# Weight panels cast in two halves, with a signal each, in a float32 kernel of three transformer blocks

## The reference

```python
x = first_block(x, p, rel_bias, ...)    # chunked mLSTM and differential attention, gated merge, conv FFN, PLE gate
x = second_block(x, l0_norm_2, ...)     # stick-breaking attention, MLA
return third_block(x, c_3, ...)         # adaLN: SwiGLU, gMLP unit and forgetting attention, SwiGLU
```

## Time and profile before

| | |
|---|---|
| median of 3 runs | 2626.04 us (2624.31 to 2631.66) |
| the profiled execution's own time | 2632.99 us |
| its span, first to last instruction | 2631.0 us |
| PE / ACT / POOL / DVE busy, share of the span | 94% / 39% / 38% / 50% |
| mean granted TensorE clock | 0.973 of 2.4 GHz |
| casts: 128 x 2048 | 188, and one of 128 x 1024 |
| POOL pieces | 754, mean 1367 ns |

### The profile page before, as it was taken

One profiled execution on the slowest core, in us unless ns is written; L12 is line 12 of the kernel. 1 busy time (PEld: TensorE's weight loads), 2 busy tenths in 40 slices (PEclk: granted clock), 3 DMA queues, 4 the chain that ended last, 5 costly groups with the idle time before them and its releaser, 6 DMA issues.

```text
span 2631.0 us, 31263 instructions
## 1 busy us (share of the span) xinstructions
PE 2477.1 (94%) x11720; PEld 1987.5 (76%) x11720; DVE 1324.2 (50%) x1870; ACT 1023.2 (39%) x1327; POOL 1007.3 (38%) x758
## 2 busy tenths in 40 slices
PE   7999899899999899998988899999989989999999
PEld 5887677688887678776766678888869657688886
DVE  6456667866667661444446662222373544522224
ACT  5445576422222543665446542222253433322222
POOL 3332244445554443222443244444424104344442
PEclk9999899999999999999989999999989998999999
DMA  3221496222222122101221122222212102122221
GB/s 137 81 75 54 167 365 261 103 96 96 96 96 96 66 84 75 49 33 50 95 96 64 35 84 96 99 99 98 96 57 93 49 17 80 48 97 96 98 99 57
DMA packets 35957, 245.52 MB, mean 93 GB/s; under 512 B 3951, under 2 KB 4079, under 8 KB 7188
## 3 DMA queue, kind: packets, MB, share of 16 engines
q1 hardware_dynamic: 30096, 207.12, 21.9%
q10 hardware_dynamic: 5764, 37.06, 3.7%
HBM read 242.06 MB, written 2.11 MB: 93 GB/s over the span
## 4 chain that ended last, share of the span: by engine, by line
issue 55%; POOL 28%; PE 15%; DVE 1%; DVEq 0%; POOLq 0%; ACT 0%; ACTq 0%
POOL WL L286 28%; PE PS L316 5%; PE PS L318 5%; PE PS L317 5%; PE PS L1030 0%; PE PS L377 0%; DVE X L2429 0%; DVE ARENA L2424 0%; POOLq L290 0%; DVEq L2095 0%; DVE ARENA L1771 0%; DVEq L2428 0%; PE PS L382 0%; DVE ARENA L1746 0%; POOLq L283 0%
## 5 line engine op out<-in xcount | busy, mean ns | idle before, releaser
L286 POOL TENSOR_TENSOR WL<-WT,WH 128x512 fp32r<-128x512 f32 x754 | 1007.1, 1367 | 1587.9 <-ACT WH L1054 1069.4
L316 PE MATMUL PS<-HH,WH 128*128 128x512 f32 x1568 | 623.2, 397 | 33.8 <-POOL WL L286 10.3
L317 PE MATMUL PS<-HL,WH 128*128 128x512 f32 x1568 | 615.7, 393 | 0.0
L318 PE MATMUL PS<-HH,WL 128*128 128x512 f32 x1568 | 615.6, 393 | 0.0
L1386 ACT CAST WH<-WT 128x2048 fp32r<-128x2048 f32 x90 | 171.9, 1910 | 603.8 <-PE PS L316 603.8
L316 PEld LDWEIGHTS PS<-HH,WH 128*128 128x128 f32 x1568 | 297.7, 190 | 110.4 <-DVE HL L1780 14.6
L316 PE MATMUL PS<-YH,WH 128*128 128x512 f32 x840 | 334.1, 398 | 24.6 <-DVE YL L2559 6.6
L318 PEld LDWEIGHTS PS<-HH,WL 128*128 128x128 f32 x1568 | 297.5, 190 | 63.6
L317 PEld LDWEIGHTS PS<-HL,WH 128*128 128x128 f32 x1568 | 297.9, 190 | 59.6 <-issue 0.2
L318 PE MATMUL PS<-YH,WL 128*128 128x512 f32 x840 | 329.9, 393 | 0.0
L317 PE MATMUL PS<-YL,WH 128*128 128x512 f32 x840 | 329.8, 393 | 0.0
(11 more groups left out here) (305 smaller groups left out, 3350.8 us busy)
## 6 DMA issues: line engine op xcount, KB each, us to landing
WT<-weights SPq DMA_DIRECT2D x188, 1024.0 KB, 4.8
ARENA<-w_ada ACTq DMA_DIRECT2D x33, 1024.0 KB, 6.8
ARENA<-w_ada SPq DMA_DIRECT2D x3, 1024.0 KB, 7.6
X<-x_fm SPq DMA_DIRECT2D x4, 512.0 KB, 7.3
out_fm<-X SPq DMA_DIRECT2D x8, 256.0 KB, 2.1
ARENA<-rel_rows ACTq DMA_DIRECT2D x1, 1024.0 KB, 5.2
CON<-constants SPq DMA_DIRECT2D x1, 640.0 KB, 11.2
WT<-weights SPq DMA_DIRECT2D x1, 512.0 KB, 5.1
```

What stands on the lines that cost most here:

```text
L286: i = nc.gpsimd.tensor_tensor(WL[s][:, e], WT[s][:, e], WH[s][:, e].bitcast(F32), ALU.subtract)
L316: i0 = nc.tensor.matmul(o, w[0], r[0], start=first, stop=False, skip_group_check=True)
L317: nc.tensor.matmul(o, w[0], r[1], start=False, stop=False, skip_group_check=True)
L318: i2 = nc.tensor.matmul(o, w[1], r[0], start=False, stop=last, skip_group_check=True)
```

## The change

Each cast becomes two casts of half the width, and each half signals `w_hi`. POOL waits twice in a panel: ahead of its first piece for 2g + 1 signals, ahead of its third for 2g + 2 (in the half-width panel 0 ahead of its first and its second). What PE, DVE and SP do is unchanged, word for word.

```diff
@@ gpsimd
             def low(g, s, width=PANEL):
-                pool.wait_ge(sem("w_hi"), g + 1)
                 for c in range(0, width, PANEL // 4):
+                    if c % (width // 2) == 0:
+                        pool.wait_ge(sem("w_hi"), 2 * g + 1 + c // (width // 2))
                     e = slice(c, c + PANEL // 4)
@@ scalar, high
-                nc.scalar.copy(WH[s][:, 0:width], WT[s][:, 0:width]).then_inc(sem("w_hi"), 1)
+                for c in (0, width // 2):
+                    nc.scalar.copy(WH[s][:, c:c + width // 2], WT[s][:, c:c + width // 2]).then_inc(sem("w_hi"), 1)
@@ scalar, hi (the FFNs' loop)
-                    nc.scalar.copy(WH[s][:, :], WT[s][:, :]).then_inc(sem("w_hi"), 1)
+                    for c in (0, PANEL // 2):
+                        nc.scalar.copy(WH[s][:, c:c + PANEL // 2], WT[s][:, c:c + PANEL // 2]).then_inc(sem("w_hi"), 1)
```

## The result

The changed kernel takes 2642.5 us (median of 13 runs, 2629.5 to 2648.2) against 2628.0 for the kernel before on the same chip (13 runs, 2624.3 to 2636.0). The ratio is 1.0040, with a 95% interval of 1.0024 to 1.0057: slower, by a little more than a measurement can tell. The forecast was 2622.4 with 2632 as its upper end, so it was wrong in size and in sign.

A forecast was written before the change was run, and what follows sets the result against it. PE was taken as the bound, busy for 2477 of 2631 us. Openings 3.9 plus MLA 0.9 minus ACT 2.2 gave 2.6 us, with 1 for clock 3.6, taking the median 2626.04 to 2622.4; range 2613 to 2632.

The forecast's parts named there:

- A panel is ready 0.75 us sooner, the second wait costs up to 0.17: Each late panel: POOL starts 0.86 us earlier, less 0.1 taken for its second wait (0 to 0.17), so ready 0.75 sooner.
- The pair ends 0.09 us later, 2.2 us in all: ACT's two half casts end 0.09 us after one whole cast would; at 25 exposed places that costs 2.2 us.
- the upper end of 4.6: Most that ACT's longer pair of casts could cost: 25 places at 0.185 us, without overlap between instructions.
- The openings, 3.9 us: PE's waits for late panels from POOL get shorter: 3.0 at four single casts, 0.6 in MERGE, 0.3 elsewhere.
- 868 and 2180: Two single late casts where PE waits 1.59 and 1.78 us for POOL; each was to gain 0.75 us.
- The opening at 520: A single late cast at 520.93 us where PE waits 2.42 us for POOL; it was to gain 0.75 us.
- 0.3 forecast for the start: Gain of 0.3 us given to the kernel's start together with the one remaining wait of PE for POOL.
- the step on MERGE: MERGE's casts are paced by DMA loads, and DVE's late handover at its end leaves only 0.6 us of gain.
- POOL against DVE, 0 us in SB: In SB POOL would now start amid DVE's subtraction; POOL waits and DVE loses nothing, so 0 us.
- The rival that ends slower by way of POOL: POOL holds up DVE instructions under way in SB and MLA, giving 2642 us; chance 0.15.
- MLA, 0.9 us: In six MLA heads POOL's earlier finish frees a colliding DVE instruction: 0.15 us a head, 0.9 us gained.
- The clock, 1 us of gain: The 3.4 us at 1.2 GHz behind the wait at 430.15 us, in MERGE, may go: 1 us gained.

The follow-up runs named there:

- e3: Kernel before with whole casts that raise the count by 2, POOL keeping the change's two waits: median 5 us up, runs 2628.0 to 2641.6 us.
- e10: Changed kernel with POOL waiting for both halves before its first piece, plus seven wide constant matmuls in the MLA heads' pause: 2630.9 us.
- e6: Kernel before with seven 512-column constant matmuls filling PE's pause ahead of L839 in the MLA heads: 2627.1 us.
- e12: Kernel before, casts untouched, with four 512-column constant matmuls once, in the wait ahead of the second MLA head's one-column matmuls: 2641.0 us.
- e13: Kernel before, casts untouched, with eight 512-column constant matmuls once, in the wait ahead of the second MLA head's one-column matmuls: 2640.4 us.
- e2: Changed kernel with halved casts kept, but POOL waiting for both halves before its first piece: as slow as the changed kernel.
- e14: Changed kernel with four 512-column constant matmuls once, in the wait ahead of the second MLA head's one-column matmuls: 2629.5 us.
- e4: Changed kernel with whole casts in panels 91 to 108, from the MLA layer's gates to its output, halves elsewhere: 2637.4 us.
- e8: Changed kernel with halves only in panels up to 90 outside the feed-forward loops, whole casts in the rest: 2636.9 us.
- e5: Changed kernel with six 512-column constant matmuls filling PE's pause ahead of L839 in the MLA heads: 2620.7 us.
- e9: Changed kernel with the same six constant matmuls issued behind the MLA heads' wait, so the pause stays: 11 us more than with the pause filled.
- e1: Changed kernel run again without any edit: five runs of 2639.2 to 2646.2 us.

## Why the prediction was wrong, step by step

- **A panel is ready 0.75 us sooner, the second wait costs up to 0.17.** Right, and a little better (0.85). The pair of casts and POOL behind it in SB:

```profile
1073.90 2.00 ACT L1056 CAST WH<-WT 128x1024 fp32r<-128x1024 f32 x2
...
1074.45 1.49 DVE L2291 TENSOR_TENSOR LBL<-ARENA,LBH 128x1280 fp32r<-128x1280 f32 x1 [1.83 <-PE PS L779]
1075.02 5.80 POOL L287 TENSOR_TENSOR WL<-WT,WH 128x512 fp32r<-128x512 f32 x4 [19.26 <-ACT WH L1056]
...
1080.11 2.37 PE L790 MATMUL PS<-ARENA 128*64 128x512 f32 x16 [0.37 <-ACT ARENA L1049]
```

  POOL starts 1.12 us after the cast's start, where it was 1.98; the second wait costs 0.01 us (e3).
- **The pair ends 0.09 us later, 2.2 us in all.** Right where it is seen: 2.00 us for the pair against 1.90 for the whole cast, and PE's wait in SB 0.37 us instead of 0.30. The total is not shown: e10 against e6 gives 3.8 us, inside the upper end of 4.6, but with the clock in it.
- **The openings, 3.9 us.** Too high. The sum of PE's gaps fell by 4.2 us, but 2.7 of them are the waits ahead of the one-column matmuls in the heads (11.2 to 8.5), which leaves some 1.5 for all the rest. By places: 868 and 2180 gave 0.92 and 0.90. The opening at 520 turned into a wait for DVE's L1826 and gave nothing, that at 1352 waits only 0.13 us less. The changed kernel is 3.3 us ahead at 150 us and 3.9 at 291, against 0.3 forecast for the start; but e6, e12 and e13, whose instructions there are those of before, are also 1.2 to 1.3 us ahead at 150, so a part is before's profiled execution. Of the lead 1.7 us are left at 478: PE now waits for DVE at MERGE's end, as the step on MERGE said.
- **POOL against DVE, 0 us in SB.** Right: L2291 still takes 1.49 us and POOL's four pieces take 5.80 instead of 5.02. It is not 0 everywhere: FFN1 loses about 1.5 us, and only where POOL starts early (not in e2). The exclusive lock of the Trainium skill's page "SBUF — State Buffer", section "SBUF: two separate sides", holds here by this row. The rival that ends slower by way of POOL named the right sign and, by chance, the right time (2642), but e2 has its loss without its mechanism.
- **MLA, 0.9 us.** The pause ahead of L839 did get shorter, from 1.52 to 1.23 us in each head, 2 us in all; a head that keeps its clock takes 16.7 us instead of 17.0. The mechanism was right: at 1462 us L2370 of 128 columns, free of POOL, takes 0.29 us where it took 1.10, and the one of 512 columns ahead of it 1.07 instead of 0.78. The term was too small.
- **The clock, 1 us of gain.** This is the step that failed. The prediction took one 3.4 us stretch behind one wait and asked whether it would go; it priced none of the others as something that could come. That stretch didn't go: it is still 3.4 us, at 434.2 instead of 431.2. The measured term is a loss: 27.3 us more at 1.2 GHz in the profiled pair, 31.8 of busy time, so about 16 us. It is larger than all the other terms together, and its sign has nothing to do with whether the change is good: 0.9 us of work in one pause turns it round in both kernels (e12, e14).

Shown is that the added time goes with more time at 1.2 GHz, that the heads' share comes and goes without any edit to their casts (e4, e8) and with 0.9 to 1.8 us of work in one pause (e12, e13, e14), and that wide matmuls by each pause take the loss away (e5, e9). Not shown is why this change brings the heads into it more often: not by their time since the kernel's start (e1), and the distance of the heads is only argued. Argued only is that the 6.0 us between 1953 and 2060 (17.1 us at 1.2 GHz against 6.8) and the 2.9 between 1569 and 1798 are of the same kind; e1 repeats both, but no run filled those places. Open is what puts one execution of the changed kernel in the lower group and the next in the upper, since no execution of the lower group was profiled; that it goes with the clock is shown by its runs (0.974 to 0.977 against 0.967 to 0.969).

## What to carry to other kernels

- Where the profile shows stretches at 1.2 GHz behind short pauses that come round in a loop, no sum of waits forecasts the time to better than what those stretches can add or take: here 14 us, for an edit whose own effect was put at under 4. Give that its own term, of both signs.
- Before such an edit is judged, put a microsecond of harmless work into one pause of the loop in both kernels. If the sign turns, as here, the comparison was of clocks. Look in the trace whether the work delays anything: here a wait took it up. Then take the sensitivity away first (here six or seven wide matmuls in a wait that is there anyway) and compare again: 2620.7 against 2627.1.
- The two groups of times, with their mean clocks, were a sign of this before any experiment.

## What the runs showed of the hardware that was not expected

- Of two pauses in the same place, the one of 1.52 us left the clock at 2.4 GHz and the one of 1.23 us was followed by 6.8 us at 1.2 GHz. What PE did ahead of the falls in the heads of these two profiles was such a pause, 1.2 to 2.0 us, and then the sixteen one-column matmuls.
- Six matmuls of 512 columns *behind* the pause kept the clock up as well as six in it (0 and 3.4 us at 1.2 GHz in the heads, from 37.6).
- An edit that takes 0.01 us a panel (e3) moved the median by 5 us, and 0.9 us of matmuls once, in a wait and without delay to what follows, moved it by 14.
- Inside the changed kernel, 0.007 less mean clock went with 13.2 us (means of its two groups, 2644.6 and 2631.4), where half of the added time at 1.2 GHz would be 18. Part of the slow stretches lies over idle time of PE: 21 us in the profile of before.
